# A hybrid decoder trunk on one core: the mixer's second half in another order, one branch for overflow jobs, output stored in four pieces

## The reference, cut to what matters

```python
xn = rmsnorm(h, mix_norm[i])
u = xn @ w_in[i]
q, k, v, lx, lg, ga, gb = split(u)
y_a = sliding_window_attention(q, k, v, bias, mask, sinks[i])
xc = causal_conv4(lx) + conv_b
r = sigmoid(block_diag(xc, w_rg) + b_rg); g = sigmoid(block_diag(xc, w_ig) + b_ig)
log_a = -8 * r * softplus(-lam);  a = exp(log_a)
s = scan over time of  s = a * s + sqrt(-expm1(2 * log_a)) * (g * xc)
y_b = s * gelu(lg)
merged = sigmoid(ga) * (y_a @ w_proj_attn[i]) + sigmoid(gb) * (y_b @ w_proj_lru[i])
h = h + merged @ w_out[i]
xn2 = rmsnorm(h, ffn_norm[i])
h = h + (swiglu(xn2) if i == 0 else moe_ffn(xn2))      # dense, then top 2 of 8 experts
xn3 = rmsnorm(h, ple_norm[i])
h = h + sigmoid(xn3 @ ple_gate_w[i]) * (p[i] @ ple_proj_w[i])
```

## Time and profile before

| | |
|---|---|
| median of 3 runs | 1723.13 us (1722.9 to 1724.54) |
| profiled execution: own time | 1724.11 us |
| profiled execution: span of the profile | 1722.1 us |
| granted PE clock, mean | 0.989 |
| DMA moved | 485.97 MB, mean 282 GB/s |

### The profile page before, as it was taken

How to read it: one execution, slowest core, us unless ns; L and a number is a source line. 1 busy time by engine, 2 the same in 40 slices (tenths; PEclk the granted TensorE clock), 3 DMA queues, 4 the chain that set the end, 5 groups by cost and what they waited for, 6 DMA issues and landing times. The chain is left out here.

```text
span 1722.1 us, 26145 instructions
## 1 busy us (share of the span) xinstructions
PE 1678.3 (97%) x10246; PEld 1306.1 (76%) x10247; DVE 1079.4 (63%) x1671; ACT 878.5 (51%) x1338; POOL 21.0 (1%) x51
## 2 busy tenths in 40 slices
PE   9999899999999999898999999999999999999978
PEld 8888899999998988896666666666666666566647
DVE  7696876665678896866554555545555455554526
ACT  6777544443456677534444544445445454454534
POOL 4000000000000000000000000000000000000000
PEclk9999999999999999998999999999999999999989
DMA  8342362643554432444999999999999999999961
GB/s 341 138 153 99 147 227 108 246 185 147 194 195 150 159 148 99 153 172 171 374 417 391 415 411 410 418 392 414 414 409 417 394 413 409 410 419 397 409 269 54
DMA packets 61887, 485.97 MB, mean 282 GB/s; under 512 B 6832, under 2 KB 9152, under 8 KB 10944
## 3 DMA queue, kind: packets, MB, share of 16 engines
q1 hardware_dynamic: 61584, 484.09, 70.4%
q10 hardware_dynamic: 176, 0.15, 0.0%
HBM read 483.15 MB, written 1.07 MB: 281 GB/s over the span
## 5 line engine op out<-in xcount | busy, mean ns | idle before, releaser
L2168 DVE TENSOR_TENSOR w_lo<-raw,w_hi 128x1024 fp32r<-128x1024 f32 x288 | 339.8, 1222 | 190.7 <-ACT w_hi L978 185.5
L483 DVE TENSOR_TENSOR w_lo<-raw,w_hi 128x1024 fp32r<-128x1024 f32 x236 | 284.4, 1220 | 109.8 <-ACT w_hi L478 108.2
L978 ACT ACTIVATE w_hi<-raw 128x1024 fp32r<-128x1024 f32 x288 | 288.2, 1050 | 55.2 <-DMA raw<-in_moe_w 55.1
L1155 PE MATMUL work<-x_r,w_hi 128*128 128x256 f32 x1024 | 298.6, 292 | 11.6 <-DVE w_lo L483 10.8
L1156 PE MATMUL work<-x_r,w_hi 128*128 128x256 f32 x1024 | 291.1, 284 | 0.0
L1157 PE MATMUL work<-x_r,w_lo 128*128 128x256 f32 x1024 | 290.8, 284 | 0.0
L478 ACT ACTIVATE w_hi<-raw 128x1024 fp32r<-128x1024 f32 x236 | 241.6, 1048 | 69.4 <-PE work L1157 29.0
L1155 PEld LDWEIGHTS work<-x_r,w_hi 128*128 128x128 f32 x1024 | 197.7, 193 | 19.7 <-issue 17.0
L1504 PE MATMUL acc<-raw,bias 128*64 128x512 f32 x768 | 204.5, 598 | 0.0
L1156 PEld LDWEIGHTS work<-x_r,w_hi 128*128 128x128 f32 x1024 | 197.9, 193 | 1.0 <-issue 0.7
L1157 PEld LDWEIGHTS work<-x_r,w_lo 128*128 128x128 f32 x1024 | 197.7, 193 | 0.0
(11 more groups left out here) (352 smaller groups left out, 2792.6 us busy)
## 6 DMA issues: line engine op xcount, KB each, us to landing
raw<-in_moe_w SPq DMA_DIRECT2D x288, 1024.0 KB, 10.5
raw<-in_mix_w SPq DMA_DIRECT2D x33, 2048.0 KB, 8.1
x<-in_moe_w SPq DMA_DIRECT2D x48, 1024.0 KB, 10.6
raw<-in_dense_w SPq DMA_DIRECT2D x21, 2048.0 KB, 8.4
raw<-in_ple_w SPq DMA_DIRECT2D x4, 2048.0 KB, 10.0
raw<-in_mix_w SPq DMA_DIRECT2D x4, 512.0 KB, 6.3
areaK<-in_ple_p SPq DMA_DIRECT2D x2, 1024.0 KB, 9.1
hT<-in_xT SPq DMA_DIRECT2D x4, 256.0 KB, 5.6
```

The source lines that it names most:

```text
L483: eng.tensor_tensor(unit(w_lo, g), raw_part(g), unit(w_hi, g).bitcast(F32), ALU.subtract).then_inc(split_ok, 1)
L978: act.activation(w_hi[n % UNITS_HELD][:, :], heavy_quarter(where, c, j), ACT.Copy).then_inc(m_hi_ok, 1)
L1155: pe.matmul(out, stat[0], move[0], start=start, stop=False, skip_group_check=True)
L2168: dve.tensor_tensor(w_lo[u][:, :], heavy_quarter(where, n // HEAVY_C, n % HEAVY_C), w_hi[u][:, :].bitcast(F32), ALU.subtract).then_inc(m_s ...
```

## The change

- ACT: `gate_b`'s sigmoid is done in two halves and six of eight slices of `gate_a`'s in a third piece, behind the evacuations of ga 4, 5 and 6, ahead of the rest of the queue there. In `gates` the last two slices of `gate_a` are left.
- DVE: `recurrence` is taken apart. `scan_input` multiplies i x xc by (a + 1) as soon as the exp is there, between the pa products; `scan` is the rest, a product and the scan; the first three scans stand in the pa loop, the others behind it, each of channels 4 to 6 followed by a split. Splits up to quarter 46 stand in the pa loop, the later ones between scans and y_b's parts.
- y_b: DVE makes the products of a pair (`made`), ACT rounds the pair (`round_yb`) after it has evacuated lg 4 to 7, and DVE takes the remainder (`yb_remainder`). Two semaphores are new.
- Overflow jobs: each engine reads only the first job's size and branches once. In the branch without a job stands the end of the expert stage (last `take_y`, `combine`, norm), with the constants of the last couple; the other branch holds the loop and the same end. `skipped` is gone. In this branch ACT splits the first two ple quarters between its copy of the heavy and of the light output, DVE splits both before its additions (before: one), and SP issues the two ple loads ahead of the last products of the experts, when their slots are free.
- The output is stored in four DMAs, each when its two slices are added.

```diff
@@ SP, behind the couples' loads
-                    with sp.Fori(0, EXTRA) as r:
-                        n = sp.value_load(extra_n[0:1, bass.ds(r, 1)], min_val=0, max_val=T)
-                        with sp.If(n > P):
+                    n = sp.value_load(extra_n[0:1, 0:1], min_val=0, max_val=T)
+                    with sp.If(n <= P):
+                        sp.wait_ge(l_used, COUPLES * LIGHT_N + 1 - 2)
+                        load((l, "ple", 0), ple_w[l, 0])
+                        sp.wait_ge(m_split, COUPLES * HEAVY_Q - 2)
+                        load((l, "ple", 1), ple_w[l, 1])
+                    with sp.Else():
+                        with sp.Fori(0, EXTRA) as r:
...
-            sp.wait_ge(h_ple, KT * DEPTH)
-            sp.dma_start(outT, hT[:, :, :]).then_inc(out_done, 16)
-            sp.wait_ge(out_done, 16)
+            for q in range(4):
+                sp.wait_ge(h_ple, KT * (DEPTH - 1) + 2 * q + 2)
+                sp.dma_start(outT[:, 2 * q:2 * q + 2, :], hT[:, 2 * q:2 * q + 2, :]).then_inc(out_done, 16)
+            sp.wait_ge(out_done, 64)
@@ ACT
+            def gate_sigmoid(l, name, gate, k0, k1):
+                for k in range(k0, k1):
+                    b, n = place[(l, name, k)]
+                    act.wait_ge(work_free[b], n + 1)
+                return act.activation(gate[:, k0:k1, :], gate[:, k0:k1, :], ACT.Sigmoid)
...
-                act.activation(gate_a[:, :, :], gate_a[:, :, :], ACT.Sigmoid).then_inc(sig_ga, 1)
+                gate_sigmoid(l, "ga", gate_a, 6, 8).then_inc(sig_ga, 1)
...
-                act.activation(gate_b[:, :, :], gate_b[:, :, :], ACT.Sigmoid).then_inc(sig_gb, 1)
-
...
+            def round_yb(l, p):
+
+                act.wait_ge(yb_made, 4 * l + p + 1)
+                act.activation(yb_hi[:, 2 * p:2 * p + 2, :], xcT[:, 2 * p:2 * p + 2, :], ACT.Copy).then_inc(yb_rounded, 1)
...
+                    if g == 2 * KT + 4:
+                        gate_sigmoid(l, "gb", gate_b, 0, 4)
+                    if g == 2 * KT + 5:
+                        gate_sigmoid(l, "gb", gate_b, 4, 8).then_inc(sig_gb, 1)
+                    if g == 2 * KT + 6:
+                        gate_sigmoid(l, "ga", gate_a, 0, 6)
...
+                    if j >= 4:
+                        round_yb(l, j - 4)
...
+                def finish(where, i, jobs):
+
+                    hi.n = first
+                    take_y(where, i, lambda: hi.to(phase_q[(l, "ple")] + 2))
+                    for k in range(KT):
+                        norm_piece(3 * l + 2, k, jobs)
+
+                with act.If(n <= P):
+                    finish("couple", COUPLES, COUPLES)
+                with act.Else():
+                    with act.Fori(0, EXTRA) as r:
                         extra(r)
...
+                    finish("extra", EXTRA, COUPLES + EXTRA)
@@ PE
+                n = pe.value_load(extra_n[0:1, 0:1], min_val=0, max_val=T)
+                with pe.If(n <= P):
+                    combine("couple", COUPLES)
+                with pe.Else():
+                    with pe.Fori(0, EXTRA) as r:
                         extra(r)
-                combine("extra", EXTRA)
+                    combine("extra", EXTRA)
@@ DVE
+            def scan(l, c):
+                dve.wait_ge(sqrt_ok, KT * l + c + 1)
+                step(dve.tensor_tensor(rT[:, c, :], rT[:, c, :], lru[:, c, CONV - 1:], ALU.mult))
+                step.settle()
+                step(dve.tensor_tensor_scan(xcT[:, c, :], decayT[:, c, :], rT[:, c, :], 0.0, ALU.mult, ALU.add))
+
+            def scan_input(l, c):
+                dve.wait_ge(decay_ok, KT * l + c + 1)
+                step(dve.scalar_tensor_tensor(out=lru[:, c, CONV - 1:], in0=decayT[:, c, :], scalar=1.0,
+                                              in1=lru[:, c, CONV - 1:], op0=ALU.add, op1=ALU.mult))
+
+            def made(l, p):
+                for j in (2 * p, 2 * p + 1):
+                    bk, n = place[(l, "lg", j)]
+                    dve.wait_ge(work_free[bk], n + 1)
+                    ins = dve.tensor_tensor(xcT[:, j, :], xcT[:, j, :], glgT[:, j, :], ALU.mult)
+                ins.then_inc(yb_made, 1)
...
-                    lo.to(phase_q[(l, "mix")] + min(36 + j + 5, 45))
+                    lo.to(phase_q[(l, "mix")] + (36 + j + 5 if j < 4 else 45 if j < 6 else 40 + j))
...
                     step(dve.tensor_tensor(lru[:, j, CONV - 1:], lru[:, j, CONV - 1:], xcT[:, j, :], ALU.mult))
-                recurrence(l)
-                step.settle()
-                for j in range(KT):
-                    lo.to(phase_q[(l, "mix")] + 44 + j + 5)
-                    bk, n = place[(l, "lg", j)]
-                    dve.wait_ge(work_free[bk], n + 1)
-                    step(dve.tensor_tensor(xcT[:, j, :], xcT[:, j, :], glgT[:, j, :], ALU.mult))
-                    if j % 2:
-                        split_pair(xcT, yb_hi, yb_lo, j - 1, yb_ok)
+                    step.settle()
+                    if j:
+                        scan_input(l, j - 1)
+                    if j == KT - 1:
+                        scan_input(l, j)
+                    step.settle()
+                    if j >= 5:
+                        scan(l, j - 5)
+                for c in range(3, KT):
+                    scan(l, c)
+                    if 4 <= c < KT - 1:
+                        lo.to(phase_q[(l, "mix")] + 44 + c)
+                step.settle()
+                made(l, 0)
+                lo.to(phase_q[(l, "mix")] + 51)
+                made(l, 1)
+                lo.to(phase_q[(l, "mix")] + 52)
+                yb_remainder(l, 0)
+                lo.to(phase_q[(l, "mix")] + 53)
+                made(l, 2)
+                yb_remainder(l, 1)
+                lo.to(phase_q[(l, "mix")] + 54)
+                yb_remainder(l, 2)
+                made(l, 3)
+                yb_remainder(l, 3)
...
+                def finish(where, i):
+
+                    lo.n = first
+                    lo.to(phase_q[(l, "ple")] + 2)
+                    for r in range(4):
+                        add_last(where, i, r)
```

More of the change, by code:

```diff
@@ L334, in trunk @@
         yb_ok = sem("yb_ok")
+        yb_made = sem("yb_made")
+        yb_rounded = sem("yb_rounded")
         merged = sem("merged")
@@ L962, in take_gathered, with take_y @@
                     act.activation(xg_hi[:, k, :], src, ACT.Copy).then_inc(m_xg_hi, 1)
-            def take_y(where, i):
+            def take_y(where, i, between=None):
                 ge(act, m_used, where, i, HEAVY_Q, HEAVY_Q, UNITS_HELD)
                 act.activation(y_sb, acc[0][:, :], ACT.Copy)
+                if between is not None:
+                    between()
                 if where == "extra":
@@ L1108, in moe @@
                 act.wait_ge(extra_ok, 1)
-                with act.Fori(0, EXTRA) as r:
-                    n = act.value_load(extra_n[0:1, bass.ds(r, 1)], min_val=0, max_val=T)
-                    with act.If(n <= P):
-                        skipped(r)
-                    with act.Else():
-                        extra(r)
-                take_y("extra", EXTRA)
-                hi.end = len(quarters)
-                hi.to(phase_q[(l, "ple")] + 2)
-                for k in range(KT):
-                    norm_piece(3 * l + 2, k)
+                n = act.value_load(extra_n[0:1, 0:1], min_val=0, max_val=T)
+                hi.end = len(quarters)
+                first = hi.n
+                def finish(where, i, jobs):
[7 more added lines that the diff above has]
+                    with act.Fori(0, EXTRA) as r:
+                        extra(r)
+                    finish("extra", EXTRA, COUPLES + EXTRA)
                 hi.to(phase_q[(l, "ple")] + 5)
@@ L2255, in moe @@
                     couple(i)
-                with dve.Fori(0, EXTRA) as r:
-                    n = dve.value_load(extra_n[0:1, bass.ds(r, 1)], min_val=0, max_val=T)
-                    with dve.If(n <= P):
-                        skipped(r)
-                    with dve.Else():
+                n = dve.value_load(extra_n[0:1, 0:1], min_val=0, max_val=T)
+                lo.end = len(quarters)
+                first = lo.n
+                def finish(where, i):
[3 more added lines that the diff above has]
+                        add_last(where, i, r)
+                with dve.If(n <= P):
+                    finish("couple", COUPLES)
+                with dve.Else():
+                    with dve.Fori(0, EXTRA) as r:
                         extra(r)
-                lo.end = len(quarters)
-                lo.to(phase_q[(l, "ple")] + 1)
-                for r in range(4):
-                    add_combined("extra", EXTRA, r)
+                    finish("extra", EXTRA)
                 for q in range(4):
```

66 lines of the change are left out of this document (20 added, 46 removed).

## The result

The kernel after takes 1692.16 us (median of 4 runs, 1691.09 to 1693.8), the kernel before 1723.74 on the same chip (1722.9 to 1724.54): ratio 0.9821, 95% interval 0.9809 to 0.9832. The forecast was 1692.4. The profiled execution took 1693.8, its span is 1691.8; before they were 1724.1 and 1722.1. So the spans differ by 30.3 us, where 30.7 were forecast.

The account below looks back on a forecast made before the run. TensorE, busy 97% of the span, bounds the kernel, so only its gaps count. Mixers 19.6 us plus tail 11.1 give 30.7 off the median 1723.1: 1692.4 us, range 1688.5 to 1699.5.

Parts of the forecast that it names:

- Part 1: Mixer gates: moving 4.8 us of ACT's table load and sigmoids to the last ga products saves 1.9 us a mixer.
- Part 2: Mixer pa to pb: recurrences ahead of remainders remove the w_lo gap and slow clock, 7.3 us a mixer, plus 0.6 at pb.
- The tight place: DVE's split for lg3: 7.4 us of work after pa7 before PE arrives at 8.7, 1.3 us spare.
- Part 3: Expert end, one branch: combine 7.5 us earlier, clock 2.4, second ple split 0.4, less 1.0 for the jump.
- upper case: Combine start: ple load takes its median 10.0 us, landing at 1665.6, so y_light is done at worst at 1668.3.
- lower case: Combine start: y_light waits only for the last expert matmul at 1666.15 and takes 0.6 us, done at 1666.8.
- the jump: Over the other branch, behind PE's combine and ahead of DVE's norm: 1.0 us lost, bounds 0 and 1.9.
- rival (a): Expert end: branches cost more, PE's gap over 2 us and a cold combine; 1696 us, chance 0.18.
- Part 4: Output in four pieces: only 256 KB stays on the path, landing in 2.1 us instead of 3.9, saving 1.8.
- (b): Mixers: one split still late at lg3 or pb2, costing 4 us a mixer; 1700 us, chance 0.12.
- (c): Expert end: ple load lands late, y_light waits for splits; four us later, clock at 0.50; 1699 us, chance 0.05.
- (d): Mixers, pa to lg: DVE needs over 2.89 us a product, PE stops before each; 1775 us, chance 0.02.

Follow-up runs that it names:

- experiment 1: Kernel after with the early sigmoids undone (gate_a's whole ahead of the recurrence gates, gate_b's whole behind them): 1696.78 us, ratio 0.9842.
- experiment 2: Kernel after with the old recurrence order (all eight channels behind the pa loop), y_b's order staying new: 1708.39 us, ratio 0.9915.
- experiment 5: Kernel after with the splits of lg3 and lg4 moved behind channel 6's scan: 1694.4 us, ratio 0.9831.
- experiment 3: Kernel after with y_b's rounding back on DVE, just ahead of each remainder: 1692.89 us, ratio 0.9822.
- experiment 6: Kernel after without the branch, overflow jobs left out on every engine: 1689.06 us, ratio 0.98.
- experiment 4: Kernel after with the output stored by one 1 MB DMA in place of four: 1693.85 us, ratio 0.9826.
- experiment 8: Kernel after with 12 idle matmuls on PE in each of two routing gaps: 1690.75 us, ratio 0.9807; profiled execution 1694.7.
- experiment 7: Kernel after with the norm and last ple written inside both branches, so engines jump only at their end: 1690.63 us, ratio 0.9809.

## Why the prediction was right

**Part 1, 1.9 a mixer.** Right: the gates' stretch, from their start to pa0, fell from 9.13 to 7.06 us, and experiment 1 gives 3.7 to 4.6 for both. The 4.8 us of ACT work found their cover.

**Part 2, 7.3 a mixer.** Right in size and cause: 10.19 less 2.88 is 7.3, in the second mixer 9.90 less 2.88 is 7.0, which the prediction took for another 7.3; experiment 2 brings the 5.2 and the slow clock back. The tight place was the named one, and its spare time (1.3 said, 1.4 by experiment 5) was right. The remaining gap ahead of pb is 0.24, where 0.1 was left of the 0.70; but the prediction reckoned with ACT's rounding as part of the new order, and experiment 3 shows that this rounding costs those 0.24 and gains nothing. In the second mixer the old gap was 0.99, so the two gaps together lost 1.2, as forecast. Both mixers: 19.45 at the routing's transposes, 19.6 forecast.

**Part 3.** The start of the combine, 7.5: 7.6 in one execution, 8.45 in the second, where the load landed earlier. In the first the load decided, as the prediction's upper case had it. In all others it did not: 0.69 to 0.77 us are the prediction's lower case, y_light's copy alone. The prediction put 1.0 us on top of that (1667.8 and not 1666.8) for a later load or for PE's reading and branching. The second costs nothing that shows (experiment 6), so this term is 0.9 too small in the usual execution. No run undoes this part by itself: the term rests on the traces, and how it divides between one branch in place of four passes and the earlier load is not shown. The clock, 2.4: right, 12.57 less the 10.24 without a jump, also by the traces alone. The second ple split, 0.4: its wait went, and the ple stage without a jump is 0.7 shorter. **The term that was mis-sized is the jump:** "bounds 0 and 1.9, I take 1.0 lost" measured 2.4 to 2.7 (2.3 to 2.9 over all executions). It failed because it counted what PE would wait and took DVE's jump for parallel; but DVE's comes after the last addition, with the norm and PE's first ple product behind it, and leaves DVE late in the stage that follows. Part of rival (a) was thus true, its jump, and part not: PE's gap stayed under 2 us and the combine at 1.00.

**Part 4, 1.8:** right, 1.86 by both traces and 1.7 by experiment 4; the 256 KB landed in 2.0, as the lower bound, the 88 KB of `col`, had it. The fit of the Trainium skill (SBUF — State Buffer, "The DMA setup-cost knee"), 2.6 by the prediction's estimate, is over what the trace shows.

The spans' 30.3 is 0.4 short of the forecast 30.7 although the jump was 1.7 too small in this execution. Most of what made up for it was not foreseen: 0.9 in the routing, where the clock fell later, 0.2 in the experts, and 0.3 more in the ple stage. The second execution (30.5) has -0.2 in the routing, 0.9 in the experts and 0.9 more at the combine instead, and 0.8 less in the mixers. These terms of under 1 us change from one execution to the next, so the closeness of the sum is in part luck; the two orders, the jump and the store stand by experiments of their own, the start of the combine and its clock by the traces.

**Rivals.** (b) was refuted as a cascade: a late split costs once, and only what goes beyond the spare time. (c) did not happen: the load landed within its range. (d) did not either: from lg0 to pb2 DVE is busy for 30.65 of 34 us, and PE waits for it 0.24. The load that (d) rested on was counted too high: from pa0 to the evacuation of lg7 DVE is busy for 37.52 of 46.26 us, not 44.1 of 46.2. Of the 16 splits counted only 13 fall into this stretch; the other three run behind y_b's last remainder.

## What to carry to other kernels

An order in a queue that makes TensorE wait costs more than its gap when the clock falls behind it (7.3 us for 5.2), and a static count of the work between two deadlines (7.4 of 8.7 us) was good to 0.1 us in the one place that was probed. A jump is priced on every engine that makes it, at the place where it stands: put it where that engine has spare time, or carry what follows into the branch. Where a cover is tight, probe it with one edit that uses it up, as experiment 5, before believing either the margin or the disaster.

## What the runs showed of the hardware

- The jump over the other branch costs DVE 2.2 to 2.7 us of standing still (2.55 and 2.25 in the two executions of the kernel after, 2.23 to 2.73 in experiments 1 to 5 and 8), PE 0.8 to 1.4; the profile files the one under another engine's result and the other under "issue". Three packets of the instruction queues fall into DVE's pause.
- PE's gap of 5.2 us was followed by 1.2 GHz each time (four gaps in the kernel before and experiment 2) and cost 1.6 to 2.6 us beyond itself; gaps of 1.5 and 1.86 never did that. In between it is open: behind the routing's gap of 2.65 the clock was 1.00 for a while in one execution, and in another of the same kernel it had fallen for these matmuls (0.59 us for two of them, not 0.39). Behind the gap of 2.73 ahead of the first expert product it was at 0.50 at once in one of the two (780.6 on), in the other a little later (1.00 in 782.3 to 783, 0.81 in 783 to 784, then 0.50). The length of the gap alone does not decide: 2.19 us were enough in experiment 8.
- Idle matmuls in a gap did not hold the clock: without them it was 1.00 up to 767.5 and 0.57 in 768 to 771, with them it stayed and then fell to 0.50 behind the next gap of 2.19, for 9 us.
- A store of 1 MB landed 3.8 us after its issue, one of 256 KB after 2.0; the last one beside packets of the instruction queues took 2.8 (experiment 7).
